# Cache attention moved out of retention's steps, and the sample's last units two a step

## What is computed

```
h = rmsnorm(x) * (1 + sc1) + sh1              # shifts, scales, gates from the conditioning
rq, rk, rv, rg, mq, mk, mv = split(h @ w_in)
# retention, chunks of 128 tokens, per head:
att = (q @ k.T) * decay;  o = att @ v + (q @ s) * q_dec;  s = s * c_dec + (k * k_dec).T @ v
ret = silu(rg) * groupnorm(o) * gn_w
# sample's attention: 3 of 16 blocks of 256 tokens per query and head, by q . mean(keys)
gate = q . mean(keys of a block);  top 3;  softmax(q @ k_sel, q @ k_own) @ v
x = x + g1 * (concat(ret, moba) @ w_out)
h2 = rmsnorm(x) * (1 + sc2) + sh2
x = x + g2 * ((silu(h2 @ w_gate) * (h2 @ w_up)) @ w_down);  y = rmsnorm(x) * final_w
```

## Time and profile before

| | |
|---|---|
| runs, us | 1021.92, 1023.32, 1020.92; median 1021.92 |
| span of the profiled execution, us | 1019.3 |
| TensorE matmul busy | 957.3 us, 94% |
| VectorE busy | 601.7 us, 59% |
| ScalarE busy | 337.1 us, 33% |
| GpSimd busy | 139.4 us, 14% |
| DMA | 269.13 MB, mean 264 GB/s |

### The profile page before, as it was taken

One profiled execution on the slowest core, in us unless ns is written; L12 is line 12 of the kernel. 1 busy time (PEld: TensorE's weight loads), 2 busy tenths in 40 slices (PEclk: granted clock), 3 DMA queues, 4 the chain that ended last, 5 costly groups with the idle time before them and its releaser, 6 DMA issues.

```text
span 1019.3 us, 20941 instructions
## 1 busy us (share of the span) xinstructions
PE 957.3 (94%) x7951; PEld 680.3 (67%) x7951; DVE 601.7 (59%) x1021; ACT 337.1 (33%) x733; POOL 139.4 (14%) x129
## 2 busy tenths in 40 slices
PE   3889999999999979899998999999999999999996
PEld 1567776766776545467756676766777777777775
DVE  1665765676576578776796674422666555453244
ACT  5411243335334426442242242432342222121113
POOL 0020113333100132224151220000000000000000
PEclk9999999999999999999998899999999999999998
DMA  9997779889777999979889579778477898787652
GB/s 340 374 354 266 275 268 314 286 268 290 260 255 229 330 373 346 370 255 329 312 304 326 173 254 285 217 215 275 120 206 204 224 232 236 217 251 246 205 188 88
DMA packets 217973, 269.13 MB, mean 264 GB/s; under 512 B 13474, under 2 KB 168426, under 8 KB 209683
## 3 DMA queue, kind: packets, MB, share of 16 engines
q1 hardware_dynamic: 111266, 127.70, 39.2%
q10 hardware_dynamic: 97392, 73.00, 23.6%
q0 software_dynamic: 9216, 67.11, 17.5%
HBM read 260.04 MB, written 5.64 MB: 261 GB/s over the span
## 4 chain that ended last, share of the span: by engine, by line
PE 76%; DVE 9%; DMA 7%; SPq 3%; issue 2%; DVEq 2%; ACT 1%; ACTq 0%
PE banks L1153 14%; PE banks L1154 13%; PE banks L1155 13%; PE banks L1106 6%; PE banks L1241 5%; PE banks L1166 4%; PE banks L1186 4%; PE banks L1168 4%; PE banks L1167 4%; DVE KT L1891 4%; DMA K<-in_cache_k,kidx 3%; DMA ctr<-in_const 1%; PE banks L1365 1%; DMA V<-in_cache_v 1%; DMA rawm<-in_w_mod 1%
## 5 line engine op out<-in xcount | busy, mean ns | idle before, releaser
L673 ACT ACTIVATE whi<-raw 128x1024 fp32r<-128x1024 f32 (+1 forms) x76 | 78.7, 1035 | 303.1 <-PE banks L1155 152.8
L1891 DVE STREAM_TRANSPOSE KT<-K 128x2048 f32<-128x2048 f32 x63 | 145.5, 2309 | 32.5 <-PE banks L1186 16.4
L1153 PE MATMUL banks<-ahi,whi 128*128 128x512 f32 x400 | 163.0, 408 | 1.0 <-DVE alo L1847 1.0
L1154 PE MATMUL banks<-alo,whi 128*128 128x512 f32 x400 | 157.1, 393 | 0.0
L1155 PE MATMUL banks<-ahi,rawlo 128*128 128x512 f32 x400 | 156.9, 392 | 0.0
L1854 DVE TENSOR_TENSOR rawlo<-raw,whi 128x1024 fp32r<-128x1024 f32 (+1 forms) x76 | 91.2, 1200 | 49.9 <-ACT whi L673 47.3
L538 POOL DMA_INDIRECT K<-in_cache_k,kidx x64 | 64.0, 1000 | 404.9 <-DVE KT L1891 357.4
L1153 PEld LDWEIGHTS banks<-ahi,whi 128*128 128x128 f32 x400 | 75.7, 189 | 30.8 <-issue 12.5
L1166 PE MATMUL banks<-ahi,whi 128*128 128x512 f32 x216 | 89.4, 414 | 1.9 <-DVE rawlo L1861 1.6
L1186 PE MATMUL banks<-KT,qbd 128*32 128x128 f32 x2048 | 74.0, 285 | 16.4 <-DVE KT L1891 14.5
L1155 PEld LDWEIGHTS banks<-ahi,rawlo 128*128 128x128 f32 x400 | 75.8, 189 | 16.8
(11 more groups left out here) (338 smaller groups left out, 1481.0 us busy)
## 6 DMA issues: line engine op xcount, KB each, us to landing
V<-in_cache_v SPq DMA_DIRECT2D x168, 256.0 KB
zT<-in_cache_v SPq DMA_DIRECT2D x56, 256.0 KB
raw<-in_w_in ACTq DMA_DIRECT2D x12, 1024.0 KB
rawm<-in_w_mod ACTq DMA_DIRECT2D x11, 1024.0 KB
raw<-in_w_gate ACTq DMA_DIRECT2D x22, 512.0 KB
raw<-in_w_up ACTq DMA_DIRECT2D x22, 512.0 KB
srw<-in_w_gate SPq DMA_DIRECT2D x22, 512.0 KB, 5.7
srw<-in_w_up SPq DMA_DIRECT2D x22, 512.0 KB, 7.3
```

The lines of the kernel that those rows point to most:

```text
L673: act.activation(whi[t % 2][:, 0:kd, :], raw[u][:, 0:kd, t % 2 * P:(t % 2 + 1) * P], ACT.Copy).then_inc(s_hi, 1)
L1153: pe.matmul(out[:, :], whi[t % 2][:, k, :], hi(k), start=(first and n == 0), stop=False)
L1154: pe.matmul(out[:, :], whi[t % 2][:, k, :], lo(k), start=False, stop=False)
L1891: dve.transpose(KTb[:, :, :, :], Kb[g % 2][:, :]).then_inc(s_kt, 1)
```

## The change

- Steps and slots are no longer the same number. `slots_of(step)` gives the slots of a step: in retention only steps 31, 34, 37 and 40 carry one (slots 30 to 33), and step 42 slot 34; from step 43 on the slot is step - 8 (BEHIND). Keys thus go on to step 71.
- From step 76 on (TWO_FROM = 68 as a slot) two slots a step are taken, which have values alone: 56 and 57, ..., 62 and 63. S_END becomes 80, in place of 76.
- Retention's order: on PE the scores stand first (pairs 0 and 1), then retention's keys turned, then the centring; in pairs 2 and 3 the keys and centring stand first. The values' part of the first of three steps and the whole third step are gone. On VectorE states stand directly behind the decayed scores, variance behind the states, and the low parts behind it. ScalarE copies the outputs into a buffer of its own (`ro_kept`) before it issues the store of the state. GpSimd's gathers are ordered anew.
- The rings of values: the one in scratch space is dropped, the last one lies where the transposed keys lay (and waits for the last keys to be multiplied), and slots 19 to 22 and 48 to 52 share one ring.
- The sample's first 12 units are done two a step (PAIRS = 6, `units_of`), with a second buffer `xtmps[1]` and two halves of `asm`; its down projection begins at step 104 in place of 106.

The diff, cut:

```diff
@@ -70,23 +70,44 @@
 R_DOWN = R_FFN + 2 * FT
-B_NORM = R_NORM // NGRP - 1
...
+SLOT_IN_RET = {NT: 28, NT + 1: 29, R_PAIR + 1: 30, R_PAIR + 4: 31, R_PAIR + 7: 32, R_PAIR + 10: 33, R_HEADS: 34}
+TWO_FROM = NG + 4
+def slots_of(step):
+    if step < NT:
+        return (step,)
+    if step < R_OUT:
+        return (SLOT_IN_RET[step],) if step in SLOT_IN_RET else ()
+    s = step - BEHIND
+    if s < TWO_FROM:
+        return (s,)
+    s += s - TWO_FROM
+    return (s, s + 1) if s < NG + LAG else ()
+B_RET = (R_OUT - BEHIND) // NGRP - 1
+B_NORM = (R_NORM - BEHIND) // NGRP - 1
...
+S_END = BEHIND + TWO_FROM + (NG + LAG - TWO_FROM) // 2
 S_OUT, S_NORM, S_FFN = S_END + 2, S_END + 6, S_END + 8
-S_DOWN = S_FFN + FT
-RING_2 = {17: 7, 18: 1, 20: 5, 21: 1, 23: 5, 24: 1, 26: 1, 27: 5}
-RING_FROM = min(RING_2)
-RING_2.update({1: 6, 3: 6})
-RING_2.update({g: 2 if g < 32 else 3 if g < 53 else 4 for g in range(29, NG, 2)})
-LANE = lambda g: 0 if g not in RING_2 else 2 if RING_2[g] in (5, 7) else 1
+PAIRS = 6
+units_of = lambda i: () if i < 0 else (2 * i, 2 * i + 1) if i < PAIRS else (PAIRS + i,) if PAIRS + i < FT else ()
+S_DOWN = S_FFN + FT - PAIRS
+RING_FROM = 17
+RING_2 = {1: 6, 3: 6, 17: 7, 18: 1, 23: 2}
+RING_2.update({g: 3 for g in range(25, 48, 2)})
+RING_2.update({g: 4 for g in range(53, NG, 2)})
+LANE = lambda g: 0 if g not in RING_2 else 2 if RING_2[g] == 7 else 1
...
@@ -267,8 +288,8 @@
     rb = at(RAWM + 1032, "rb", [P, T])
     rings = [VB, [raw[1][:, 2 * i:2 * i + 2, :].rearrange("p a c -> p (a c)") for i in range(4)],
              [zT[:, RK + i, :] for i in range(4)], [zT[:, RG + i, :] for i in range(4)],
-             [at(B["K"] + ROWS * W + W * i, f"V{4 + i}", [P, W]) for i in range(4)],
-             [scr[:, 0, :], scr[:, 1, :], free[:, 0, :], free[:, 1, :]],
+             [at(B["KT"] + W * i, f"V{4 + i}", [P, W]) for i in range(4)],
+             None,
              [zT[:, RQ + i, :] for i in range(4)],
              [rawm[:, 2 * i:2 * i + 2, :].rearrange("p a c -> p (a c)") for i in range(4)]]
...
-            if g == 29:
+            if g == 23:
                 sp.wait_ge(s_ra, HP)
-            if g == 33:
+                sp.wait_ge(s_kt1, HP)
+            if g == 25:
                 sp.wait_ge(s_hlo, 2 * KT)
             if g == 53:
-                sp.wait_ge(s_kt, NG)
+                sp.wait_ge(s_lg, NG)
             for s in range(4):
...
@@ -589,21 +612,32 @@
         pool.wait_ge(s_hi, 1)
         gather(0)
         gather(1)
-        for g in range(2, NG):
+        def next_keys(g):
             pool.wait_ge(s_kt, g - 1)
             gather(g)
+        for g in range(2, R_PAIR):
+            next_keys(g)
             if M_TURN <= g - 4 < M_TURN + 2 * HP:
                 if g - 4 == M_TURN:
                     pool.wait_ge(s_const, 32)
                 rotate(g - 4)
-            if g > R_PAIR and (g - R_PAIR - 2) % 3 == 0 and g <= R_PAIR + 11:
-                queries_decayed((g - R_PAIR - 2) // 3)
-            if g in (R_PAIR + 7, R_PAIR + 10, R_PAIR + 13):
-                scale_heads((g - R_PAIR - 7) // 3)
-            if g == R_PAIR + 3:
-                pool.wait_ge(s_hrs, 1)
-                heads = mobatok.rearrange("p i (h d) -> p i h d", h=H)
-                pool.tensor_tensor(heads, heads, gain[:, 4:8, 0:8].unsqueeze(3).broadcast_to((P, TT, H, HD)), ALU.mult).then_inc(s_hm, 1)
+        next_keys(30)
+        next_keys(31)
+        queries_decayed(0)
+        pool.wait_ge(s_hrs, 1)
+        heads = mobatok.rearrange("p i (h d) -> p i h d", h=H)
+        pool.tensor_tensor(heads, heads, gain[:, 4:8, 0:8].unsqueeze(3).broadcast_to((P, TT, H, HD)), ALU.mult).then_inc(s_hm, 1)
+        next_keys(32)
+        for hp in range(1, HP):
+            queries_decayed(hp)
+            next_keys(32 + hp)
+            scale_heads(hp - 1)
+        for g in range(R_OUT + 1, NG + BEHIND):
+            next_keys(g - BEHIND)
             if g in (R_NORM + 3, R_NORM + 4):
                 for k in range(4):
                     scale_x(4 * (g - R_NORM - 3) + k)
...
                 for k in (2 * hp, 2 * hp + 1):
                     stage_block_heads(k, KT + k - 4)
-            if hp:
-                keep_heads(hp - 1)
-            if hp == 1:
-                keep_x(2)
-            if hp == 3:
-                act.wait_ge(s_vd, 4 * 27)
-                next_chunk(0)
-                keep_x(5)
             act.wait_ge(s_kt1, hp + 1)
             if hp == 0:
                 act.wait_ge(s_const, 48)
...
+            if hp == 1:
+                keep_x(2)
+            if hp == 2:
+                act.wait_ge(s_vd, 4 * 19)
+                next_chunk(0)
+            if hp == 3:
+                keep_x(5)
             if hp >= 2:
                 for k in (2 * hp, 2 * hp + 1):
                     stage_hi(k, KT + k - 4)
             slot(s + 1)
...
-                keep_x(0)
                 act.wait_ge(s_hri, 1)
                 act.activation(gain[:, 4:8, 0:8], gain[:, 4:8, 0:8], ACT.Sqrt).then_inc(s_hrs, 1)
+                keep_x(0)
...
-            if hp == 0:
-                keep_x(1)
             if hp == 2:
...
                 act.activation(gates, gates, ACT.Silu).then_inc(s_sg, 1)
                 act.wait_ge(s_sev, NIN + 2)
                 act.activation(zs[:, ZRG:ZRG + W], zs[:, ZRG:ZRG + W], ACT.Silu).then_inc(s_ssg, 1)
             if hp == 3:
-                keep_x(7)
-                act.wait_ge(s_vd, 4 * 28)
                 split_out(0)
                 stage_hi(0, KT + 4)
                 stage_hi(1, KT + 5)
             act.wait_ge(s_ro, hp + 1)
+            act.activation(ro_kept[:, :], SB[:, :], ACT.Copy).then_inc(s_roe, 1)
             act.dma_start(ret_prompt[0, 0].rearrange("h d v -> (h d) v")[hp * P:(hp + 1) * P, :], sst[:, 3, :]).then_inc(s_rs, 16)
-            act.activation(scr[:, 3, :], SB[:, :], ACT.Copy).then_inc(s_roe, 1)
+            if hp in (0, 2, 3):
+                keep_x({0: 1, 2: 4, 3: 7}[hp])
...
-                act.wait_ge(s_vd, 4 * 52)
+                act.wait_ge(s_vd, 4 * 48)
             if n == 8:
                 act.wait_ge(s_state, 32)
             if n == 10:
-                act.wait_ge(s_lg, NG)
-            if n == 11:
+                act.wait_ge(s_kt, NG)
+            if n == 12:
                 act.wait_ge(s_vd, NPAGE * NB_SEQ)
             if n == 14:
                 act.wait_ge(s_oe, NB_SEQ)
...
@@ -1482,24 +1525,7 @@
                 last = pe.transpose(HEADS_IN[k][:, i * P:(i + 1) * P], src[:, k % 4, i * P:(i + 1) * P], ident)
             last.then_inc(s_xt, 1)
-        for hp in range(HP):
-            s = R_PAIR + 3 * hp
-            slot_head(s)
-            if hp:
-                turn_out(hp - 1)
-            if hp == 1:
-                block_gates(s // NGRP - 1)
-                turn_x(2)
-            if hp == 3:
-                turn_x(5)
-            slot_values(s)
-            if hp == 0:
-                pe.wait_ge(s_rk, 2 * HP)
-                pe.wait_ge(s_vt2, 12)
-                pe.wait_ge(s_on, 16)
-            for c in range(TT):
-                last = pe.transpose(SB[:, c * P:(c + 1) * P], zT[:, RK + hp, c * P:(c + 1) * P], ident)
-            last.then_inc(s_kt1, 1)
+        def ret_scores(hp):
             if hp >= 2:
                 pe.wait_ge(s_stg, KT + 2 * hp - 2)
             for c in range(TT):
@@ -1508,15 +1534,36 @@
                     last = pe.matmul(bank[h2][:, c * P:(c + 1) * P], zT[r:r + 64, RK + hp, c * P:(c + 1) * P],
                                      zT[r:r + 64, RQ + hp, c * P:(c + 1) * P], start=True, stop=True)
             last.then_inc(s_ra, 1)
-            slot_tail(s)
+        def turn_ret_keys(hp):
+            if hp:
+                pe.wait_ge(s_roe, hp)
+            for c in range(TT):
+                last = pe.transpose(SB[:, c * P:(c + 1) * P], zT[:, RK + hp, c * P:(c + 1) * P], ident)
+            last.then_inc(s_kt1, 1)
+        for hp in range(HP):
+            s = R_PAIR + 3 * hp
+            if hp == 0:
+                pe.wait_ge(s_rk, 2 * HP)
+                pe.wait_ge(s_vt2, 12)
+                pe.wait_ge(s_on, 16)
+            if hp < 2:
+                ret_scores(hp)
+                if hp == 1:
+                    turn_x(2)
+                turn_ret_keys(hp)
+                if hp:
+                    turn_out(hp - 1)
+            else:
+                turn_ret_keys(hp)
+                turn_out(hp - 1)
+                ret_scores(hp)
+            if hp == 3:
+                turn_x(5)
+                block_gates(B_RET)
             slot_head(s + 1)
-            if hp == 0:
-                turn_x(0)
-            if hp == 1:
-                turn_x(3)
-            if hp == 3:
-                turn_x(6)
             slot_values(s + 1)
             pe.wait_ge(s_kt2, hp + 1)
             if hp:
@@ -1527,21 +1574,13 @@
                     last = pe.matmul(DB[r:r + 64, c * HD:(c + 1) * HD], scr[:, 3, c * P + r:c * P + r + HD],
```

(72 more changed lines are left out.)

112 lines of the change are left out of this document (63 added, 49 removed).

## The result

| kernel | median us | runs | ratio to the kernel before, 95% interval |
|---|---|---|---|
| before | 1021.81 | 4 | |
| changed | 1052.16 | 4 | 1.028 [1.0247, 1.0312] |

The change makes the kernel 2.8% slower; the forecast was 1026 us, range 1013 to 1036. The part that was to gain did gain, and more than forecast. Three places lost more than forecast: one had been priced at nothing, one near nothing and one at half. Medians and ratios leave out three executions in a slower state, one of the kernel before (1191.84 us, beside the experiments), one of e6 (5100.85) and one of e7 (2300.59); with theirs e6 and e7 have 1030.43 and 1029.07 us, the first of which an expectation quotes.

What follows compares the result with a forecast made beforehand. TensorE was taken as the bound (busy 957.3 of 1019.3 us), retention held by cache traffic and VectorE. Terms -23.9 + 18.5 + 1.0 + 8.6 = +4.2 us gave 1026 us, 8-in-10 range 1013 to 1036.

Steps and rivals of the forecast that it cites:

- Part 1: Slots leaving retention: the stretch falls from 85.6 to 61.7 us by a hand-laid order, -23.9 us.
- rival B: Retention takes its lower bound, 55 us, making the kernel 1019 us; chance 0.20, alone or with another rival.
- The wait between pairs 2 and 3: In retention, PE waits 2.3 us for ScalarE's copy of the outputs, queued behind two SiLUs.
- DMA share: Sign in retention: the share of the DMA engines, 0.97 before, falls well below 0.9.
- Steps 43 to 62: Steps 43 to 63 keep their form and cost nothing.
- Part 2: Keys, values and small matmuls moved behind retention, where PE has no idle time, are paid in full: +18.5 us.
- Part 3: Cache and weight traffic in steps 64 to 79 costs +1 us, bounds 0 and 8.
- rival C: Steps 64 to 79: keys, values and weights exceed what the DMA engines carry, +7 us more, 1033 us; chance 0.13.
- Part 4: Two sample units a step, from step 88: late weights and VectorE's product cost +8.6 us, bounds 0 and 12.
- Late weights: Between steps 88 and 93 the sample's weights land 1.0 or 3.4 us late, 7.8 us in all.
- VectorE's product: With two units a step VectorE's product comes late, hidden by the late weights but once: 0.8 us.
- The gain at the end: The sample ends two steps earlier, 117 in place of 119 of 121, and nothing waited for it: 0.

Runs made afterwards that it cites:

- e6: Changed kernel with the edits of e3, e4 and e5 in one: 1029.58 us, ratio 1.0077 to the kernel before.
- e7: Changed kernel with the edits of e3, e5 and e2 in one, six doubled units kept: 1028.66 us, ratio 1.0056.
- e3: Changed kernel with the store of the sample's retention state cut into 8, one a step in steps 62 to 69, and x_sample's load issued first: 1044.83 us.
- e10: Changed kernel with the edits of e3, e4 and e9 in one: 1029.16 us, ratio 1.0059 to the kernel before.
- e12: Changed kernel with e9's page numbers read ahead and e1's light values: 1042.06 us, ratio 1.0206.
- e9: Changed kernel with SyncE reading the page numbers of slots 56 to 63 ahead, before waiting for the pages' places: 1043.0 us, ratio 1.0181.
- e1: Changed kernel with value loads of slots 58 to 63 bringing 16 of 128 rows of each page, as many loads issued: 1052.59 us.
- e2: Changed kernel with the weights of the sample's units 2 to 11 loaded for 16 of 128 partitions, as many loads issued: 1048.25 us.
- e8: Kernel before with only the sample's first twelve units done two a step (steps 84 to 89): 1038.37 us, ratio 1.0156.
- e4: Changed kernel with two units a step only in steps 88 and 89 (PAIRS = 2 in place of 6): 1045.7 us, ratio 1.019.
- e5: Changed kernel with the fourth page of each of value slots 58 to 63 loaded from GpSimd's queue instead of SyncE's: 1045.29 us, ratio 1.0226.

## Why the prediction was wrong

**What bounds it.** Right: what was put behind retention was paid in full. But "PE busy all the time" said only that nothing was late yet, not how much room each queue had left.

**Part 1, forecast -23.9.** Mechanism right, size too small, mis-sized by some 5 us: -28.7 here, -26 to -29.5 over all profiles with the edit (slot 29's keys to the first tile 60.5 to 64.0 us; 89.9 and 90.0 in the two without it). Window against window it is 56.9 us, against 61.7 in the hand-made order, and 56.2 to 59.7 over all profiles, so rival B's end of the range (55) was nearly right. The wait between pairs 2 and 3 was foretold at 2.3 and is 2.4. DMA share 0.71, below 0.9 as said. Steps 43 to 62 at nothing: within what executions differ by.

**Part 2, forecast +18.5.** Right to 1 us (17.8, as follows). With the waits taken away, step 63 with its keys is 1.6 us longer than before (e3), steps 64 to 75 12.0 (e10) and steps 76 to 79 6.8 (e12): 20.4, of which steps 69 and 72 still hold 2.6 us of waiting for values (by the weight loads' waits in e10). A step's keys cost 1.2 us (6.66 to 7.88), not 1.0. PE's busy time in e10 is 955.4 us against 957.3: the work is the same.

**Part 3, forecast +1: the step that failed first.** Measured some 15 in two places, besides 4 of waits in steps 64 to 75.
In steps 76 to 79 I had priced SyncE's issues at 0.91 us each, "7.3, beneath the step's 7.9, and the last page just makes it". The 0.91 was four issues' 3.63 us divided by four, as in this line of SyncE's in the kernel before:
```profile
607.85 3.63 SPq L423 DMA_DIRECT2D V<-in_cache_v  x4
```
But such a group runs from the first start to the last end: it is three intervals of 1.10 and one issue of 0.33. Eight loads are 8.8 us, more than the step, and because a slot's pages wait for the values two slots before, none can be issued early. That cost 6.1 us (e9), and when it was gone the bytes showed behind it, 3.6 us more (e12), 9.7 together. Bytes alone, without the issues, gave 2.0 (e1). So rival C named the right stretch and half the right cause; its argument against itself, that 606 to 629 had no wait, was true of a stretch with one slot a step.
In step 63 I wrote that steps 43 to 63 keep their form and cost nothing. The form was kept; what stands beside it was not. The store sits in ScalarE's queue in both kernels, and its price, 6.98 us of a blocked ScalarE, was in the trace before. The last keys were transposed before that block ended (617.91 us), and PE had no idle time from 615.8 to 630.8 us. The change takes that cover away and puts a gather of keys beside the same transfers; the block was 12.60 us and 7.2 on the path, 5.6 of them without the keys' work (14.3 to 8.7 in e3, whose time fell by 7.3). I asked which work moves, and not which idle engine's wait the moved work would now stand behind.

**Part 4, forecast +8.6: the term that was mis-sized.** The stretch is 24.3 us longer; 6.9 is work brought forward, 17.4 is loss (11.1 to 17.4 over the six profiles). Late weights, forecast 7.8, are 12.8 (e2; 6.5 to 12.8 over the six), VectorE's product, forecast 0.8, is 4.6. The rate taken from the earlier trace rows, 290 GB/s, was right, but as that of one queue at a time, not of both together. What the working left out: three times SyncE's own issue for the second buffer is held 2.3 to 3.5 us, while ScalarE's queue moves the prompt's weights, so the next reload starts late too; the backlog runs on into step 94, where there is one unit again and which is still 2.7 us too long; and PE, idle in between, is granted 0.91 of its clock, where it has 1.00 with light weights. I had let the delay of one pair hide that of the next; it was carried on instead. e8 shows a like price in the kernel before, 21.8 us in the stretch and +15.9 us of time (12.5 to 19.3) with the work given back.

**The gain at the end, forecast 0.** It is 2.8 us, 2.4 of them in steps 116 and 117, which have no piece of the sample's down projection any more; PE is full there. Nothing had to wait for the sample for that.

**The sum.** Without the two rows that executions scatter by (+6.0 and -3.3): retention -28.7, work moved behind it +17.8 (20.4 less the waits of steps 69 and 72), these waits 2.6 and another 1.5 in the changed kernel's own steps 64 to 75, step 63 5.6, page loads 9.7, the units' stretch 24.3, and -0.4 and -2.8 of the last rows: +29.6, the measured difference without these two rows. The losses in it that belong to parts 3 and 4 are 2.6 + 1.5 + 5.6 + 9.7 + 17.4 = 36.8, where the forecast had 9.6. This sum closes by the way it is made, of stretches of the same profiles. The test that doesn't depend on it is that the times of e3, e4 and e9, taken together, give e10's.

What stays open: with the three mends (e10) the kernel is 6.0 us slower than before (3.0 to 9.1), though its profiled execution's span is only 1.2 us longer; its runs spread over 15 us, those of the kernel before beside them over 13, and which stretch makes the slower ones slow no profile here shows. No version here beats the kernel before.

## What to carry to other kernels

Take the rate of an issuing engine from start to start, never from a group's length divided by its count, and compare it with the step before you double the transfers of a step. Look in the trace of before for issues that last longer than an issue should: each is an engine that stands still in a full queue, harmless only as long as nothing late stands behind it, and moved work may put something there. A stretch that PE fills completely shows nothing of the reserves of its feeders; before filling it further, add up each queue's own seconds.

## What the runs showed of the hardware

Issuing one DMA behind a 1 MB store in pieces under 512 B held ScalarE for 12.60 us in the changed kernel, and 6.98 us in the kernel before, where no gather ran beside it; issued ahead of the store it took 3.28 us, and the store's eight pieces 0.39 to 0.99 us each (e3). Reading a page number from memory into a register and then issuing its load took SyncE 1.10 us a page, 0.52 with the number read ahead. A page of 32 KB was still waited for until 4.6 us after its issue (e1: last issue at 745.62, the matmul on it at 750.25); a whole page of 256 KB in the same place until 5.4 us after it (changed kernel: 743.48, 748.86). A page load issued from GpSimd took it 0.54 to 0.58 us and was in time (e5). One queue alone moved 290 GB/s in pieces of 512 B and 375 in pieces of 1 KB (kernel before, 837.6 to 839.8 and 975.5 to 977.5 us).
